# Ten places for gathered expert rows in all four tiles, with the stick-breaking core's buffers laid into the choice's buffers

## The chip, the cores and the metric

The kernel runs on one core of one Trainium2 chip. The metric is the device time of one execution in microseconds (us); smaller is better. The core has TensorE (PE), VectorE (DVE), ScalarE (ACT), GpSimd (POOL) and SyncE (SP), which run their own instruction streams and meet through semaphores, and 16 DMA engines that all queues share.

## The reference, cut to what matters

Two transformer blocks stand one behind the other, on one sequence of 256 tokens with 1024 features. The first (band attention, a short convolution, a gated feed-forward part, two layers) isn't touched. The second has two layers as well: an mLSTM mixer in layer 0, stick-breaking attention in layer 1, and behind each mixer a layer of retrieved experts:

```python
def peer_ffn(h, w_q, sub_keys, peer_u, peer_v):      # for each block of 128 tokens
    q = einsum('td,de->te', xb, w_q)                 # 8 heads x 2 halves x 128
    s = einsum('thpk,pnk->thpn', q, sub_keys)        # scores of 2 x 128 keys
    s_top, i_top = top_k(s, 16)
    cand = s_top[0][:, None] + s_top[1][None, :]     # 16 x 16 candidates
    g_top, pos = top_k(cand, 16); expert = cand_idx[pos]
    u, vv = peer_u[expert], peer_v[expert]           # 16384 experts, 1024 floats each
    act = gelu(einsum('thkd,td->thk', u, xb))
    return einsum('thk,thkd->td', softmax(g_top) * act, vv)
```

So each token takes 8 x 16 = 128 experts in each of the two layers. The stick-breaking mixer computes, for 16 heads, z = q k, log(1 - sigmoid(z)) summed over the later keys, and a = exp(log sigmoid(z) + that sum), which weighs v.

## The kernel before

**Tiles and rows.** There are two blocks of 128 tokens and two layers, so four tiles: tile 0 and 1 are layer 0, tile 2 and 3 are layer 1. A tile has 128 picks (`PICKS`). Pick q of the whole program (0 to 511) means: GpSimd gathers for each of 128 tokens one row of 2048 floats (u and v of one expert side by side, 8 KB) by an indirect DMA (L1718); VectorE multiplies the u half with the token's row and sums it (`dot`, L2457); ScalarE makes the gelu, multiplies it with the softmax weight and writes a diagonal matrix (L1530, L1533, L1539), two picks at a time; TensorE multiplies the diagonal with the v half and adds it up in PSUM (`weighted`, L1124).

**Places.** A gathered row lies in a place until TensorE has used it. `ROW[q]` says which one. Places 0 to 3 are `ring_b`, 4 to 7 are `ring_a`, the upper half of the weight ring `wring`. In tile 0 there are two more, 8 and 9: `spare`, and the first half of `qp0`, a buffer of queries that is free by then. They exist in tile 0 only: `spare` and `qp0` are allocated in an early stack that is closed and overlaid by the buffers of the second layer's mixer, among them `az`, `sp_`, `ls` and `ex` of 4 KB a partition each. So tile 0 has ten places and tiles 1 to 3 have eight. `EARLIER[q]` is the pick that had the place before; GpSimd waits for `rows_free` to reach it (L1715), then issues. GpSimd does nothing else at this time.

**What runs beside the rows.** The rows of tile 0 run beside the end of layer 0 and the choice of tile 1's experts. The second layer comes in two passes (`second_layer(t)`, in the text first and second pass), one for each block of tokens. The first pass runs beside the rows of tile 1 and ends with the choice for tile 2; the second runs beside the rows of tile 2 and ends with the choice for tile 3. Tile 3's rows run alone. A pass is: a norm; six slabs of weights for k, v and q (`tile_rows`, L1144); the norm of the heads; the core, in which groups of heads go through scores (TensorE), logarithms (ScalarE) and sums (VectorE and TensorE); two slabs of w_out, one right behind the other; a norm; four slabs of w_q (L1238); the scores of the keys (L998, copied to `sc` at L1677); and the choice (`choose`: the maxima L2362, indices L2367, and so on), all on VectorE. The 16 heads go through the core in 4 groups in the first pass and in 8 in the second.

**The order of the work** is written by hand. `PLAN` gives for each step of a pass the number of picks by which dots (VectorE, `picks`), gelus (ScalarE, `gelus`) and products (TensorE, `weighted`) must have come before the engine goes on with the next step. An engine thus waits for a row when the plan's count asks for one that hasn't landed. The plan of tile 1: 2 picks before the norm, 3 at each of the six slabs, 24 in the core, 3 + 3 around w_out, 2 before the next norm, 3 at each slab of w_q, 5 before the choice and 41 inside it; the plan of tile 2 has 40 in the core, 2 instead of 3 at w_out and w_q, and 31 in the choice. The indices of the next tile's first 64 picks are ready halfway through the choice, those of the other 64 at its end; GpSimd waits for them (`chosen`) before pick 0 and 64 of a tile.

**Weights.** The slabs of the second layer (2 MB each) go by SP's queue into the two lower places of `wring` (L541); a load is issued when the slab two before it has been used. They take the same DMA engines as the gathers.

**The buffers of the change.** `cand` (8 heads x 256 candidates, 8 KB a partition) and `sc` (16 x 128 scores, 8 KB) are used from the copy of the queries (`qpt` is a view of `cand`, L1673) to the end of the choice. `az`, `sp_`, `ls`, `ex` are used from the pass's first norm (`hkT` is a view of `ex`) to the end of the core; `krow` and `qrow` are views of `sp_` and `ls`. ScalarE writes eight diagonals in turn (`DIAGS`).

Of the kernel before, what the change touches and what calls it, by code (L numbers as in the profile page):

```python
# [8 lines left out]
F32 = mybir.dt.float32  # L9
# [8 lines left out]
P = 128  # L18
D = 1024
SEQ = 256  # L20
NT = SEQ // P
KC = D // P
DEPTH = 2
# [55 lines left out]
PICKS = PEER_HEADS * TOPK  # L79
RING = 8  # L80
HALF_RING = RING // 2


TEN, EIGHT = (0, 1, 2, 3, 8, 9, 4, 5, 6, 7), (6, 7, 0, 1, 2, 3, 4, 5)
ROW = [TEN[q % 10] if q < PICKS else EIGHT[q % RING] for q in range(DEPTH * NT * PICKS)]
EARLIER = [[p for p in range(max(0, q - 10), q) if ROW[p] == ROW[q]][-1:] for q in range(len(ROW))]
TURN = [ROW[:q + 1].count(ROW[q]) for q in range(len(ROW))]
PART = 2
LAST = DEPTH * NT * PICKS - 1
# [72 lines left out]
def build(nc, ins, out):  # L162
    ctx = ExitStack()
    with ctx:
# [6 lines left out]
        def sb(name, shape, dt=F32, stack=ctx):  # L171
            return stack.enter_context(nc.sbuf_tensor(name, shape, dt))
# [121 lines left out]
        def se(name, shape, dt=F32):  # L294
            return sb(name, shape, dt)
# [3 lines left out]
        cand = se("cand", [P, PEER_HEADS, TOPK * TOPK])  # L299
        sc = se("sc", [P, 2 * PEER_HEADS, NKEYS])  # L300
# [19 lines left out]
        def row(q):  # L320

            r = ROW[q]
            if r == RING:
                return spare[:, :]
            if r > RING:
                return qp0[:, 0].rearrange("p h n -> p (h n)")
            return (ring_b, ring_a)[r // HALF_RING][:, r % HALF_RING, :]

        early = ExitStack()
        sc1 = sb("sc1", [P, 2 * PEER_HEADS, NKEYS], F32, early)  # L330
        qp0 = sb("qp0", [P, NT, 2 * PEER_HEADS, P], F32, early)
        spare = sb("spare", [P, 2 * D], F32, early)
        early.close()

        qpt = cand[:, :, :].rearrange("p h (a n) -> p (h a) n", a=2)
# [2 lines left out]
        def sk(name, shape, dt=F32):  # L338
            return sb(name, shape, dt)
# [4 lines left out]
        vrow = sk("vrow", [P, NT, D])  # L344
        skT = sk("skT", [P, KC, SEQ])
        srs, sss = sk("srs", [P, SB_HEADS]), sk("sss", [P, SB_HEADS])
        az, sp_, ls, ex = [sk(n, [P, 2, 512]) for n in ("az", "sp_", "ls", "ex")]


        hkT = ex[:, :, :].rearrange("p a n -> p (a n)").rearrange("p (k n) -> p k n", n=P)  # L350
# [214 lines left out]
        def _(pe):  # L565
# [549 lines left out]
            def weighted(tt, k, late=True):  # L1115

                while multiplied_rows[0] < tt * PICKS + (multiplied(k) if late else k):
                    q = multiplied_rows[0]
                    multiplied_rows[0] += 1
                    if q % PICKS == 0 and tt:  # L1120
                        pe.wait_ge(sums_read, tt)
                    pe.wait_ge(diag_ready, q + 1)
                    for half in range(2):
                        m = nc.tensor.matmul(pr[half][:, :], diag[:, q % DIAGS, :], row(q)[:, D + half * 512:D + (half + 1) * 512],  # L1124
                                             start=(q % PICKS == 0), stop=(q % PICKS == PICKS - 1))
                        if q == LAST and half == 0:
                            m.then_inc(sums_full, 1)
                    m.then_inc(rows_free, 1)
                if k == PICKS:
                    pe.drain().then_inc(sums_full, 1)  # L1130
# [559 lines left out]
        @block.gpsimd  # L1690
        def _(pool):
            pool.wait_ge(w_in_slot[0], 16)
            pool.dma_start(mask8[:, :, :], ins["c_mask8"]).then_inc(const_in, 16)
            pool.dma_start(cs[:, :, :, :], ins["c_cs"]).then_inc(const_in, 16)
            pool.dma_start(adab[:, :], ins["ada_bias"]).then_inc(adab_in, 16)
            pool.wait_ge(c_ready, 1)

            with pool.Fori(0, ADA_CHUNKS // 2) as i:
                for a in range(2):
                    pool.wait_ge(ada_free, 2 * i + a + 1)  # L1700
                    pool.sem_inc(wait_seen, 1)
                    pool.dma_start(aring[:, a, :], ins["ada_rows"][bass.ds(2 * i + a, 1)].rearrange("a p n -> p (a n)")).then_inc(ada_in[a], 16)  # L1702

            for tt in range(DEPTH * NT):
                for p in range(PICKS):
                    q = tt * PICKS + p
                    if q == TEN.index(9):
                        pool.wait_ge(sc_ready, 4)
                    for r in range(2):
                        if q == TEN.index(HALF_RING + 2 * r):  # L1710
                            pool.wait_ge(w_free, S2 + SLOTS_B - 3 + r + R)
                    for i, (_, h0, _) in enumerate(CHOICES[tt]):
                        if p == h0 * TOPK:
                            pool.wait_ge(chosen, CHOICES_BEFORE[tt] + i + 1)
                    for p0 in EARLIER[q]:  # L1715
                        pool.wait_ge(rows_free, p0 + 1)
                    pool.sem_inc(wait_seen, 1)
                    pool.indirect_dma_start(out=row(q), out_offset=None, in_=ins["peer_uv"],  # L1718
                                            in_offset=bass.IndirectOffsetOnAxis(ap=eidx[:, tt % NT, p:p + 1], axis=0)).then_inc(row_in[ROW[q]], 16)


        @block.vector
        def _(dve):
# [730 lines left out]
            def dot(q):  # L2454

                dve.wait_ge(row_in[ROW[q]], 16 * TURN[q])
                m = nc.vector.tensor_tensor_reduce(out=row(q)[:, 0:D], in0=row(q)[:, 0:D], in1=hrow[:, q // PICKS % NT, :], scale=1.0,  # L2457
                                                   scalar=0.0, op0=ALU.mult, op1=ALU.add, accum_out=dots[:, q % PICKS:q % PICKS + 1])
                if q % PART == PART - 1 or q >= PAIRED:
                    m.then_inc(dots_ready, 1)  # L2460
# [208 lines left out]
```

## Time and profile before

| what | value |
|---|---|
| runs of the kernel before | 2644.65 us median of 3 (2629.52 to 2653.48) |
| profiled execution | span 2638.4 us from first to last instruction, 6.25 us under that median; no separate time of it is given |
| TensorE, VectorE, ScalarE, GpSimd busy | 88%, 66%, 37%, 26% of the span |
| gathers (software queue) | 90000 packets, 595.97 MB |
| HBM read | 824.95 MB, 313 GB/s over the span |
| tile 0's rows | from about 1155 us |
| first pass, second pass, tile 3 alone | 1511 to 1908, 1908 to 2320, 2320 to 2630 us |

The profile is of one execution; all times in rows are us from its start. PE is TensorE's matmuls, PEld its weight loads. In a row of the timeline the bracket holds how long the engine was idle before the instruction and what ended the idle time. The chain of waits is followed back from the last instruction, at each step to what released it or to the instruction before it on its engine. The granted clock of TensorE was 0.983 of full speed over the span.

### The profile page before, as it was taken

The numbers are of one execution on the slowest core, as the hardware profiler recorded it, in microseconds if no ns is written. First come the engines' busy times: TensorE is split into PE (matmuls) and PEld (weight loads), VectorE is DVE, ScalarE is ACT, GpSimd is POOL, SyncE is SP. The second block draws the span as 40 slices with busy tenths as digits, with TensorE's granted clock in tenths as the row PEclk, the third lists the DMA queues.
The fourth block names the chain that finished last, engine by engine and source line by source line (L and its number), as shares of the span: only waits on it lengthen the run. The fifth ranks groups of instructions, "written<-read, shape, count | busy, mean of one in ns | idle before, by whom it ended". The sixth has DMA issues, their size and how long they took to land.

```text
span 2638.4 us, 33375 instructions
## 1 busy us (share of the span) xinstructions
PE 2328.1 (88%) x11926; PEld 1622.5 (61%) x11926; DVE 1728.6 (66%) x3439; ACT 972.9 (37%) x2088; POOL 682.4 (26%) x631
## 2 busy tenths in 40 slices
PE   8999999999999999898877799987798999777777
PEld 7999999899999979785322244463343446232222
DVE  5687677768677767666975555547954654954444
ACT  4444433453443345322322224413324732322222
POOL 0000001000000100023545433324423333455543
PEclk9999999999999999999999999999999999899999
DMA  7545477664547754169999999999999998999998
GB/s 298 199 160 196 163 277 282 249 246 155 193 148 279 284 196 160 68 236 382 403 419 422 421 411 391 401 390 407 413 401 373 395 395 325 383 412 421 422 421 354
DMA packets 110513, 828.14 MB, mean 314 GB/s; under 512 B 14384, under 2 KB 15296, under 8 KB 30992
## 3 DMA queue, kind: packets, MB, share of 16 engines
q0 software_dynamic: 90000, 595.97, 56.1%
q1 hardware_dynamic: 20352, 230.08, 23.2%
q8 instruction: 94, 1.54, 0.2%
q14 instruction: 67, 0.55, 0.1%
HBM read 824.95 MB, written 1.05 MB: 313 GB/s over the span
## 4 chain that ended last, share of the span: by engine, by line
PE 54%; DMA 18%; DVE 14%; ACT 5%; issue 4%; POOL 1%; DVEq 1%; ACTq 1%; PEldq 0%; SPq 0%; PEld 0%; POOLq 0%
PE pd L573 16%; PE pr L1124 12%; PE pa L573 11%; DMA ring_b<-in_peer_uv,eidx 9%; DMA wring<-in_peer_uv,eidx 6%; PE pr L573 6%; PE pa L1144 3%; DVE ring_b L2457 3%; PE pa L1238 2%; DVE wring L2457 2%; DVE wring_r L1774 1%; PE pd L1144 1%; DMA wring<-in_w_mix 1%; ACT junk L1539 1%; DMA aring<-in_ada_rows 1%
## 5 line engine op out<-in xcount | busy, mean ns | idle before, releaser
L1124 PE MATMUL pr<-ring_b,junk 128*128 128x512 f32 x976 | 464.2, 622 | 112.2 <-ACT junk L1539 111.6
L1124 PE MATMUL pr<-wring,junk 128*128 128x512 f32 x968 | 451.4, 611 | 105.2 <-ACT junk L1539 99.8
L1718 POOL DMA_INDIRECT ring_b<-in_peer_uv,eidx x244 | 294.4, 1207 | 597.1 <-PE pr L1124 348.3
L2457 DVE CUSTOM_DVE_ANT_0 wring<-wring,hrow 128x1024 f32<-128x1024 f32 x242 | 293.7, 1223 | 218.9 <-DMA wring<-in_peer_uv,eidx 210.9
L2457 DVE CUSTOM_DVE_ANT_0 ring_b<-ring_b,hrow 128x1024 f32<-128x1024 f32 x244 | 295.8, 1224 | 201.6 <-DMA ring_b<-in_peer_uv,eidx 195.3
L1124 PEld LDWEIGHTS pr<-ring_b,junk 128*128 128x128 f32 x976 | 184.3, 197 | 373.9 <-issue 197.2
L1124 PEld LDWEIGHTS pr<-wring,junk 128*128 128x128 f32 x968 | 178.3, 192 | 360.8 <-issue 188.1
L1718 POOL DMA_INDIRECT wring<-in_peer_uv,eidx x242 | 291.8, 1206 | 417.3 <-PE pr L1124 359.1
L1530 ACT ACTIVATE gel<-dots 128x2 f32<-128x2 f32 x255 | 51.6, 203 | 657.2 <-DVE dots L2457 655.4
L1702 POOL DMA_DIRECT2D aring<-in_ada_rows x112 | 60.2, 538 | 871.1 <-DVE adal L1867 870.9
L573 PE MATMUL pd<-hhi,wring_r 128*128 128x256 f32 x1024 | 222.1, 281 | 0.0
L1774 DVE TENSOR_TENSOR wring_r<-wring,wtop 128x2048 fp32r<-128x2048 f32 (+1 forms) x78 | 176.4, 2263 | 58.0 <-ACT wtop L1268 55.4
L1774 DVE TENSOR_TENSOR wring_r<-wring,wring_r 128x2048 fp32r<-128x2048 f32 (+1 forms) x77 | 173.8, 2262 | 36.0 <-ACT wring_r L1268 33.3
L1539 ACT ACTIVATE junk<-ident,gel 128x128 f32<-128x128 f32 x510 | 176.8, 394 | 18.4 <-issue 1.0
L1268 ACT CAST wring_r<-wring 128x2048 fp32r<-128x2048 f32 x80 | 149.3, 1883 | 71.0 <-DMA wring<-in_w_mix 28.7
L1268 ACT CAST wtop<-wring 128x2048 fp32r<-128x2048 f32 x80 | 148.9, 1881 | 67.1 <-DMA wring<-in_w_back 25.4
L573 PEld LDWEIGHTS pd<-hhi,wring_r 128*128 128x128 f32 x1024 | 170.7, 189 | 0.0
L573 PE MATMUL pa<-flo_b,wring_r 128*128 128x256 f32 x768 | 166.9, 284 | 0.0
L1867 DVE CUSTOM_DVE_ANT_0 aring<-aring,crow 128x1024 f32<-128x1024 f32 x112 | 136.5, 1219 | 12.3 <-DMA aring<-in_ada_rows 12.0
L573 PEld LDWEIGHTS pa<-flo_b,wring_r 128*128 128x128 f32 x768 | 128.7, 190 | 4.0 <-issue 4.0
L1533 ACT ACTIVATE gel<-gel,wexp 128x1 f32<-128x1 f32 x510 | 122.7, 287 | 18.7 <-issue 1.4
L573 PE MATMUL pd<-hhi,wtop 128*128 128x256 f32 x384 | 108.6, 283 | 2.9 <-DVE hlo_r L1817 2.9
(393 smaller groups left out, 4358.7 us busy)
## 6 DMA issues: line engine op xcount, KB each, us to landing
wring<-in_w_mix SPq DMA_DIRECT2D x38, 2048.0 KB, 8.7
aring<-in_ada_rows POOLq DMA_DIRECT2D x112, 512.0 KB, 5.3
wring<-in_w_stick SPq DMA_DIRECT2D x24, 2048.0 KB, 9.4
wring<-in_w_ffn SPq DMA_DIRECT2D x22, 2048.0 KB, 8.7
wring<-in_w_lstm SPq DMA_DIRECT2D x12, 2048.0 KB, 8.3
wring<-in_w_back SPq DMA_DIRECT2D x8, 2048.0 KB, 8.5
wring<-in_w_back SPq DMA_DIRECT2D x4, 1536.0 KB, 6.8
ring_b<-in_peer_uv,eidx POOLq DMA_INDIRECT x244
```

The lines of the kernel that those rows point to most:

```text
L573: m = nc.tensor.matmul(out_, lhsT, rhs, start=start, stop=stop)
L1124: m = nc.tensor.matmul(pr[half][:, :], diag[:, q % DIAGS, :], row(q)[:, D + half * 512:D + (half + 1) * 512], start=(q % PICKS == 0), stop ...
L1144: i = nc.tensor.matmul(b[:, :], src(k), wring[:, m % R2, k, :], start=(k == 0), stop=(k == KC - 1))
L1238: i = nc.tensor.matmul(b[:, c * P:(c + 1) * P], wring[:, m % R2, k, c * P:(c + 1) * P], hT[:, k, cut], start=(k == 0), stop=(k == KC - 1))
L1268: nc.scalar.copy(hi, raw).then_inc(whi_ready, 1)
L1533: nc.scalar.activation(gel[:, i:i + 1], gel[:, i:i + 1], ACT.Copy, scale=wexp[:, g * PART // PICKS % NT, i // TOPK, i % TOPK:i % TOPK + 1])
L1539: nc.scalar.activation(diag[:, q % DIAGS, :], ident[:, :], ACT.Copy, scale=gel[:, q % PICKS:q % PICKS + 1]).then_inc(diag_ready, 1)
L1702: pool.dma_start(aring[:, a, :], ins["ada_rows"][bass.ds(2 * i + a, 1)].rearrange("a p n -> p (a n)")).then_inc(ada_in[a], 16)
L1718: pool.indirect_dma_start(out=row(q), out_offset=None, in_=ins["peer_uv"], in_offset=bass.IndirectOffsetOnAxis(ap=eidx[:, tt % NT, p:p + 1 ...
L1774: nc.vector.tensor_tensor(lo, raw, hi, ALU.subtract).then_inc(wlo_ready, 1)
L1867: nc.vector.tensor_tensor_reduce(out=aring[:, j % 2, :], in0=aring[:, j % 2, :], in1=crow[:, :], scale=1.0, scalar=0.0, op0=ALU.mult, op1= ...
L2457: m = nc.vector.tensor_tensor_reduce(out=row(q)[:, 0:D], in0=row(q)[:, 0:D], in1=hrow[:, q // PICKS % NT, :], scale=1.0, scalar=0.0, op0=A ...
```

## The change

All tiles use ten places. Place 8 is the second half of a new buffer `ring_c` and place 9 its first half, except in tile 0, where place 9 stays in `qp0`. `ring_c` takes the 16 KB a partition where the four core buffers lay; these become views of `cand` (`az`, `sp_`) and `sc` (`ls`, `ex`), each with the shape it had. `spare` goes. `ROW` now turns through the ten places over all 512 picks, and each pick's predecessor is the one ten before; nothing else is changed, no wait and no plan count.

```diff
@@ -81,9 +81,10 @@
-TEN, EIGHT = (0, 1, 2, 3, 8, 9, 4, 5, 6, 7), (6, 7, 0, 1, 2, 3, 4, 5)
-ROW = [TEN[q % 10] if q < PICKS else EIGHT[q % RING] for q in range(DEPTH * NT * PICKS)]
-EARLIER = [[p for p in range(max(0, q - 10), q) if ROW[p] == ROW[q]][-1:] for q in range(len(ROW))]
+TEN = (0, 1, 2, 3, 8, 9, 4, 5, 6, 7)
+PLACES = len(TEN)
+ROW = [TEN[q % PLACES] for q in range(DEPTH * NT * PICKS)]
+EARLIER = [[q - PLACES] if q >= PLACES else [] for q in range(len(ROW))]
 TURN = [ROW[:q + 1].count(ROW[q]) for q in range(len(ROW))]
@@ -321,15 +322,14 @@
             r = ROW[q]
             if r == RING:
-                return spare[:, :]
+                return ring_c[:, 1]
             if r > RING:
-                return qp0[:, 0].rearrange("p h n -> p (h n)")
+                return qp0[:, 0].rearrange("p h n -> p (h n)") if q < PICKS else ring_c[:, 0]
             return (ring_b, ring_a)[r // HALF_RING][:, r % HALF_RING, :]
 
         early = ExitStack()
         sc1 = sb("sc1", [P, 2 * PEER_HEADS, NKEYS], F32, early)
         qp0 = sb("qp0", [P, NT, 2 * PEER_HEADS, P], F32, early)
-        spare = sb("spare", [P, 2 * D], F32, early)
         early.close()
@@ -344,7 +344,15 @@
         srs, sss = sk("srs", [P, SB_HEADS]), sk("sss", [P, SB_HEADS])
-        az, sp_, ls, ex = [sk(n, [P, 2, 512]) for n in ("az", "sp_", "ls", "ex")]
+        ring_c = sk("ring_c", [P, 2, 2 * D])
+
+        def pair_in(v, i):
+
+            h = v[:, i * v.shape[1] // 2:(i + 1) * v.shape[1] // 2, :]
+            return h.rearrange("p (a h) n -> p a (h n)", a=2)
+
+        az, sp_ = pair_in(cand, 0), pair_in(cand, 1)
+        ls, ex = pair_in(sc, 0), pair_in(sc, 1)
```

## Rows read from the trace of the kernel before

**Rows 1.** Page, part 2: GB/s moved in each of 40 slices of 66 us.
```profile
GB/s 298 199 160 196 163 277 282 249 246 155 193 148 279 284 196 160 68 236 382 403 419 422 421 411 391 401 390 407 413 401 373 395 395 325 383 412 421 422 421 354
```

**Rows 2.** Windows: stretch; PE, PEld, DVE, ACT, POOL busy us; PEclk, DMA share, GB/s.
```profile
1375.00:1500.00 125.00, 92.51 (x200) 35.93 (x200) 61.66 (x100) 34.10 (x125) 62.68 (x50) 1.00 1.01 421
1500.00:2325.00 825.00, 719.54 (x2208) 356.25 (x2208) 516.51 (x1252) 290.46 (x804) 301.57 (x260) 0.97 0.97 391
2325.00:2600.00 275.00, 207.57 (x447) 81.29 (x448) 136.21 (x223) 76.31 (x277) 141.45 (x112) 0.99 1.01 421
```

**Rows 3.** Windows, same columns: two stretches in which fewer bytes come.
```profile
2195.00:2225.00 30.00, 29.79 (x178) 22.24 (x178) 9.74 (x27) 8.71 (x26) 6.47 (x7) 1.00 0.70 249
2275.00:2300.00 25.00, 20.80 (x40) 8.11 (x38) 23.90 (x101) 8.33 (x23) 12.03 (x10) 0.86 0.87 319
```

**Rows 4.** Chain of waits, 1500 to 2325: start us, us, what; all transfers.
```profile
1485.20 17.53 DMA wring<-in_peer_uv,eidx
...
1616.92 8.38 DMA ring_b<-in_peer_uv,eidx
...
1706.08 9.99 DMA wring<-in_peer_uv,eidx
...
1797.81 9.24 DMA ring_b<-in_peer_uv,eidx
...
1817.74 11.68 DMA ring_b<-in_peer_uv,eidx
...
1870.87 9.08 DMA wring<-in_peer_uv,eidx
...
2154.43 9.26 DMA ring_b<-in_peer_uv,eidx
...
2233.59 12.25 DMA wring<-in_peer_uv,eidx
```

**Rows 5.** Timeline, first pass, after w_out: DVE waits, then PE waits.
```profile
1713.64 1.23 DVE L2457 CUSTOM_DVE_ANT_0 wring<-wring,hrow 128x1024 f32<-128x1024 f32 x1 [6.68 <-DMA wring<-in_peer_uv,eidx]
...
1720.86 1.54 PE L903 MATMUL pd<-ident,xn 128*128 128x128 f32 x6 [5.28 <-DVE xn L2166]
```

**Rows 6.** Timeline at the start of the choice: first pass, then second.
```profile
1789.75 0.58 ACT L1677 COPY sc<-pa 128x512 f32<-128x512 f32 x1 [0.31 <-PE pa L998]
...
1792.78 1.23 DVE L2457 CUSTOM_DVE_ANT_0 wring<-wring,hrow 128x1024 f32<-128x1024 f32 x1 [7.06 <-DMA wring<-in_peer_uv,eidx]
...
1793.93 1.25 DVE L2362 MAX8 top<-sc 128x8 f32<-128x128 f32 x6
...
2219.08 0.58 ACT L1677 COPY sc<-pa 128x512 f32<-128x512 f32 x1 [0.31 <-PE pa L998]
...
2221.26 1.64 DVE L2362 MAX8 top<-sc 128x8 f32<-128x128 f32 x8
```

**Rows 7.** Waits of DVE, 1793 to 1910, then 2221 to 2325: us, times, longest.
```profile
DVE wring L2457 <- DMA wring<-in_peer_uv,eidx: 9.2, 5, 7.1
...
DVE ring_b L2457 <- DMA ring_b<-in_peer_uv,eidx: 1.7, 4, 0.8
...
DVE wring L2457 <- DMA wring<-in_peer_uv,eidx: 6.4, 2, 6.1
...
DVE ring_b L2457 <- DMA ring_b<-in_peer_uv,eidx: 1.1, 2, 0.7
```

**Rows 8.** Timeline of DVE at the start of the first core.
```profile
1625.33 1.23 DVE L2457 CUSTOM_DVE_ANT_0 ring_b<-ring_b,hrow 128x1024 f32<-128x1024 f32 x1 [1.22 <-DMA ring_b<-in_peer_uv,eidx]
```

**Rows 9.** Chain of waits in the last tile's rows: one transfer.
```profile
2391.62 12.56 DMA ring_b<-in_peer_uv,eidx
```

**Rows 10.** Weight loads (L541): landing times; then PE around the second pass's w_q.
```profile
DMA to landing us min/median/max: 7.9/9.4/12.8
...
2178.89 3.70 PE L1124 MATMUL pr<-ring_b,junk 128*128 128x512 f32 x8
...
2193.36 7.31 PE L1238 MATMUL pa<-hT,wring 128*128 128x128 f32 x64
```

## The prediction, as it went on record before the changed kernel ran

> **What bounds the kernel now.** The page comes first. Its bytes per slice [rows 1] show where the change acts: from the 19th slice on, when experts' rows are gathered, the core moves 325 to 422 GB/s, and no slice passes 422. I read this as a ceiling of the transfers with dips under it. The windows say how deep the dips are [rows 2]. In the first of its three stretches (tile 0, ten places) and in the third (the last tile alone, eight places) the rate is 421 GB/s. Between them, in the 825 us in which the two passes of the second layer run beside tiles 1 and 2, it is 391. A row gather moves 128 rows of 2048 floats, 1.049 MB, so one takes 2.49 us at 421 GB/s. If the middle stretch ran at 421, it would be (421 - 391) / 421 x 825 = 58.8 us shorter. That is the ceiling of anything that only keeps the transfers busier.
>
> The ceiling is not what more places bring. The chain of waits says which wait ended last [rows 4]: between 1500 and 2325 us it holds eight transfers, and all the rest is TensorE, VectorE and ScalarE. The first one belongs to tile 0. From 1880 to 2154 us none is on the chain at all: there the rows lie ready before they are used. So the middle stretch is mostly bound by the engines, whose work is interleaved with the rows by the plan's counts, and the missing 30 GB/s are mostly the transfers waiting for a free place. In the last tile it is the other way: all of its rows come at 2.49 us each, and the end is set by when the last gather lands.
>
> **What a place is worth.** A place is busy from the issue of its gather until TensorE has multiplied its row. Under the ceiling eight places make a turn of 8 x 2.49 = 19.9 us, of which 12.56 are the transfer [rows 9]; ten make 24.9 us, of which 17.53 are the transfer (the first row of [rows 4]). The rest, some 7.3 us, is the same. So in a stretch that the transfers bound, ten places give a longer queue and no more rows per second: that is what rows 2 show side by side. Two more places help only around a stretch in which TensorE or VectorE is late: the transfers can then run two rows further ahead, which is worth at most 2 x 2.49 = 5.0 us each time the work turns from engine-bound to transfer-bound.
>
> **The change part by part.**
>
> Tile 0 keeps its ten places and its order; only one address moves. 0 us. Rows 128 to 133 have rows ten earlier as their predecessors before and after, so the turn to tile 1 gains nothing.
>
> The shared buffers: no instruction, wait or DMA is added or taken away, and the four core buffers keep their shapes. The choice of the next experts and the core of the same pass are ordered by engine queues already. Cost 0; nothing queues behind anything new. Had a hidden order been broken, waits would be needed that the diff doesn't have.
>
> (a) After w_out in the first pass. Two slabs run on TensorE back to back with no rows between, all eight places fill, and VectorE then needs the ninth and tenth row for its plan: it sits 6.68 us for the first of them, and TensorE 5.28 us for the norm behind them [rows 5]. Both rows would be in the two added places. VectorE's wait goes; TensorE, which multiplies older rows until then, is next to be late, so the gain is its 5.28: **5.3 us**. Bounds: 0 if TensorE takes longer over the rows it now has in hand, 6.7 if it too starts earlier.
>
> (b) Before the choice in the first pass VectorE waits 7.06 us for a row and starts the maxima at 1793.93, while the scores were there at 1789.75 + 0.58 = 1790.33 [rows 6]. With the row issued two places sooner the scores are next: **3.5 us** (0 to 3.6).
>
> (c) The same place in the second pass: 2221.26 - (2219.08 + 0.58) = **1.6 us** (0 to 1.6) [rows 6].
>
> (d) Inside the two choices, where VectorE is the busy engine, it still waits for rows: 9.2 - 7.1 + 1.7 = 3.8 us and 6.4 - 6.1 + 1.1 = 1.4 us [rows 7], the longest one being that of (b) and (c). VectorE is close to being the bound, and part of what it gains is waited for later. I take half of 5.2: **2.6 us** (0 to 5.2).
>
> (e) The cores. The one transfer on the chain there ends in a wait of 1.22 us [rows 4, 8]. **1.2 us** (0 to 5.0, two rows).
>
> (f) The turn into the last tile. From 2275 to 2300 us the transfers move 319 GB/s, so they idle (421 - 319) / 421 x 25 = 6.1 us [rows 3] because all places are taken. With two more they fetch two rows in that time, and since nothing but transfers bounds what follows, the end comes 2 x 2.49 = **5.0 us** earlier (0 to 5.0). This is the surest term.
>
> Elsewhere the dips are engine-bound on both sides; the deepest, 2195 to 2225 us at 249 GB/s with TensorE busy 29.79 of 30 us [rows 3], can't get shorter.
>
> Sum: 5.3 + 3.5 + 1.6 + 2.6 + 1.2 + 5.0 = 19.2 us. The profiled execution has a span of 2638.4 us; the median of the three runs shown is 2644.65, 6.25 us above. 2638.4 - 19.2 = 2619.2 for a span, and 2644.65 - 19.2 = **2625.5 us** for the time (0.7% less). About 1% is what a measurement of this kernel can tell from no change, so this would be hard to see.
>
> **The rivals.**
>
> 1. *Hidden anyway* (0.25). The engines' chain has other waits of nearly the same length beside each row wait, so (a) to (e) vanish and at most (f) stays: a gain of 0 to 5, time 2640 to 2645. For it: TensorE is busy 720 of the 825 us [rows 2]. Against: at (a) and (b) both the waiting and the next-late engine are visible. The same result follows if the transfers themselves can't do more in the middle stretch than they do: then the time is 2645. Against it: 421 GB/s held for 125 and for 275 us [rows 2].
> The Trainium skill ("SBUF — State Buffer", section "A bandwidth-pool intuition that's wrong") puts the HBM side at about 358 GB/s per core. By that rule 391 would be past the limit already, and no extra place could bring anything; the trace disagrees, with 421 GB/s on this one core.
>
> 2. *Every dip shrinks* (0.17). If the engines' stages are themselves held up by rows throughout, each dip loses up to two rows. From 58.8 take what two rows can't cover: the stretch 2195 to 2225 idles 30 x (421 - 249) / 421 = 12.3 us, so 7.3 remain, and 1.1 of the 6.1 us at 2275. Gain 50, time about 2594. Against: only seven transfers of this stretch are on the chain.
>
> 3. *Slower: the weights come late* (0.05). Each 2 MB slab shares the transfers with the rows in flight, and more rows would be ahead of it. Room is least around w_q in the second pass: a slab is freed at 2178.89 and its successor needed at 2193.36, 14.5 us, and the longest landing of any slab is 12.8 us [rows 10]. If slabs waited behind all rows in flight, ten would make 24.9 + 5.0 = 29.9 us, 15.4 too late for two slabs: +31 us, 2676. It decides from a landing of 14.5 us on. Against: by the same reckoning eight places would give 24.9 us now, and the longest is 12.8.
> The Trainium skill ("DMA: Bandwidth & Descriptors", section "Queues, rings and completion order") says that each DMA engine takes turns between its queues, a packet at a time. By that rule a deeper gather queue doesn't push the slabs back, the price is 0 and the time stays at the sum; the landings of 7.9 to 12.8 us agree.
>
> 4. *It doesn't do what it says* (0.03): the rows come in the old rhythm because something else (the index choice for the next tile, the eight diagonals) holds the gathers; time 2645.
>
> **How the numbers follow.** The forecast, a gain of 12 to 28 us, gets 0.50; the rivals 0.25, 0.17, 0.05 and 0.03. The 1% bound lies at 26.4 us: faster by more is rival 2 and the upper edge of the forecast, 0.22. Slower by over 1% is rival 3 and a little for what I can't see, 0.05. The rest, 0.73, is within 1%. The range 2600 to 2648 takes in the forecast (2617 to 2633), rival 1, and the nearer part of rival 2.
>
> **What would show it.** Right: the middle stretch runs at 396 to 402 GB/s, with the last tile still at 421; the transfer in a saturated turn takes about 17.5 us in all tiles; TensorE's 5.28 us wait for the norm is gone and the maxima start within 0.5 us of the last score copy; the window of 25 us before the last tile moves over 400 GB/s; slab landings stay under 14 us. Wrong: the 6.68 and 7.06 us waits are still there (rival 4) or gone without the stage getting shorter (rival 1), TensorE waits for slabs (rival 3), or the middle stretch is over 30 us shorter (rival 2).

## The result, and the profile after

| | before | after |
|---|---|---|
| runs | 2639.44 us median of 20 (2629.52 to 2657.13) | 2617.75 us median of 20 (2609.43 to 2635.95) |
| ratio after / before | | 0.9923, 95% interval 0.9907 to 0.9939 |
| profiled execution, span | 2638.4 us | 2611.3 us |

The change gains 0.77%, 20.3 us of 2639.4 by the ratio, between 16 and 25 us by its interval. The forecast was a gain of 19.2 us. The two profiled executions differ by 27.1 us in span. That is more than the runs say. Executions of one kernel differ with the granted clock (of the 20 of after, the fastest took 2609.43 us at 0.989 and the slowest 2635.95 at 0.976; one of e_plan10, below, with 3883.59 us at 0.553, is left out of its ratio). So the stages below are used for where the time went, and the ratio for how much.

The page after, part 2, GB/s in each of 40 slices, now 65 us long:

```profile
GB/s 298 204 159 201 162 282 282 241 237 160 191 165 271 271 237 162 33 224 369 401 418 422 421 422 410 417 409 414 421 424 390 395 392 347 418 398 421 422 422 353
```

Against [rows 1] the ceiling is the same, 424 at most, and the slices from the 24th to the 30th have filled up: 390 to 413 before, 409 to 424 now. The deep dip near the end (325 before) is still there (347). The three stretches of [rows 2], after; the columns are the same:

```profile
1375.00:1500.00 125.00, 92.19 (x200) 35.74 (x199) 61.65 (x100) 34.44 (x125) 63.57 (x50) 1.00 1.01 421
1500.00:2300.00 800.00, 705.82 (x2202) 350.60 (x2201) 511.23 (x1246) 288.69 (x798) 304.98 (x260) 0.98 0.98 404
2300.00:2575.00 275.00, 207.71 (x453) 81.47 (x452) 139.58 (x229) 78.44 (x285) 147.56 (x114) 1.00 1.01 421
```

The outer stretches stay at 421 GB/s. The middle one moves the same bytes (391 x 825 and 404 x 800 agree within 0.2%) in 25 us less, with nearly the same number of instructions (2202 products for 2208). Its busy TensorE time falls by 13.7 us, more than six products of less than half a us each explain, and its granted clock is 0.98 instead of 0.97. That last pair is not in the forecast, and comes back below.

The chain of waits after, 1500 to 2330 us, all of its transfers (start us, us):

```profile
1800.85 14.63 DMA wring<-in_peer_uv,eidx
...
1851.45 14.67 DMA wring<-in_peer_uv,eidx
...
2311.69 11.15 DMA wring<-in_peer_uv,eidx
```

Seven transfers of [rows 4] after tile 0's have become three, two in the first choice and one at the turn into the last tile. The one that is gone from the second pass, issued at 2154.43 in [rows 4], comes back below too. In the last tile a transfer takes 17.5 us where it took 12.56 [rows 9], as in tile 0 before: one row of the same view, 2340 to 2500 us.

```profile
2355.02 17.52 DMA wring<-in_peer_uv,eidx
```

**Where the time went.** I cut each profiled execution at the starts of named instructions and took the differences, in us. A stage in which nothing changed still comes out 1.7 or 3.4 us apart now and then: from the first to the last of the six slabs of the second pass it is 67.5 or 70.9 us, with one value in between, in an order that has nothing to do with the places (eight places have 70.9, but also 67.5). The rows show what the steps are. The same rows' products, behind the same wait of 2.01 us for a diagonal, in before and then in after:

```profile
1954.89 5.40 PE L1124 MATMUL pr<-wring,junk 128*128 128x512 f32 x8 [2.01 <-ACT junk L1539]
```

```profile
1941.41 3.70 PE L1132 MATMUL pr<-ring_b,junk 128*128 128x512 f32 x8 [2.01 <-ACT junk L1547]
```

Before has 5.40 us twice in these slabs, at a granted clock of 0.89 over 1945 to 1960 us and 0.88 over 1974 to 1988; after has 3.70 both times, at 1.00. From 1500 us on each of the two traces has six such waits of 2.01 us; a slow stretch follows three of them in before and one in after. So about 1.7 us behind such a wait are there in one execution and not in another, and a single difference of that size needs a row behind it.

In the table "nine", "twelve late" and "six" are e_nine, e_twelve and e_six of the experiments.

| stage | eight (before) | eight (e_layout) | nine | ten (after) | twelve late | six |
|---|---|---|---|---|---|---|
| pass 1: last w_out slab to first w_q slab | 37.2 | 38.1 | 33.3 | 30.3 | 30.2 | 40.7 |
| pass 1: first core scores to the next slab | 64.9 | 64.9 | 64.9 | 64.9 | 64.9 | 73.4 |
| pass 1: last w_q slab to first maxima | 20.9 | 21.6 | 19.1 | 17.4 | 17.4 | 26.0 |
| first choice, to tile 1's last sum | 114.5 | 117.2 | 116.6 | 113.1 | 113.5 | 132.0 |
| pass 2: core | 110.0 | 110.0 | 110.0 | 110.0 | 110.0 | 119.4 |
| pass 2: last w_out slab to first w_q slab | 29.3 | 29.2 | 27.3 | 27.3 | 27.2 | 35.9 |
| pass 2: first to last w_q slab | 34.5 | 34.5 | 32.9 | 32.9 | 32.9 | 32.9 |
| pass 2: key scores to first maxima | 6.0 | 5.9 | 4.5 | 4.5 | 4.5 | 13.4 |
| second choice, to tile 2's last sum | 99.0 | 99.4 | 98.2 | 97.3 | 98.9 | 100.3 |
| last tile, to its last sums | 312.9 | 313.0 | 310.5 | 308.0 | 303.0 | 351.7 |

Before against after: 6.9, 0, 3.5, 1.4, 0, 2.0, 1.6, 1.5, 1.7 and 4.9 us. That is 23.5 of the 27.1, and 3.2 more than the ratio gives; 3.4 are the scatter of the second pass's six slabs, 2.0 lie ahead of tile 0's end, where nothing differs, and the rest, of either sign, is spread over the other stages.

Three places, seen in rows. TensorE after w_out in the first pass, of after (start us, us):

```profile
1709.88 3.60 PE L1132 MATMUL pr<-ring_b,junk 128*128 128x512 f32 x8
1713.32 1.04 PE L911 MATMUL pd<-ident,xn 128*128 128x128 f32 x8
1714.19 3.60 PE L1132 MATMUL pr<-ring_b,junk 128*128 128x512 f32 x8
```

and of before, at the same place, with the row of the products that follow:

```profile
1720.86 1.97 PE L903 MATMUL pd<-ident,xn 128*128 128x128 f32 x8 [5.28 <-DVE xn L2166]
1722.61 4.28 PE L1124 MATMUL pr<-wring,junk 128*128 128x512 f32 x8
```

(L1132 is L1124 of before, L911 is L903.) The wait of 5.28 us is gone. But so are 0.9 us of the norm's products and 0.7 of the rows' (1.97 to 1.04, 4.28 to 3.60). The window 1720 to 1723 us of before shows the granted clock at 0.59:

```profile
1720.00:1723.00 3.00, 2.15 (x9) 2.10 (x10) 2.96 (x4) 0.00 (x0) 0.00 (x0) 0.59 0.99 412
```

After 5.28 us of idleness the engine goes on for part of these 3 us at the lower of its two levels (1.2 instead of 2.4 GHz, half speed). The gap costs 5.28 + 1.6 = 6.9 us.

ScalarE's last score copy and VectorE's first maxima in the first pass, of after:

```profile
1780.75 0.58 ACT L1685 COPY sc<-pa 128x512 f32<-128x512 f32 x1 [0.31 <-PE pa L1006]
1781.41 1.65 DVE L2370 MAX8 top<-sc 128x8 f32<-128x128 f32 x8 [3.88 <-ACTq L1686]
```

The maxima start 0.08 us after the copy's end, where they started 3.6 later [rows 6]. VectorE still idles 3.88 us, but now for the scores and no longer for a row.

The second pass, where I had named no gain: TensorE from the rows' products to the first w_q slab, of before, then the slab of after.

```profile
2163.22 3.70 PE L1124 MATMUL pr<-wring,junk 128*128 128x512 f32 x8 [0.64 <-ACT junk L1539]
2166.76 1.04 PE L991 MATMUL pa<-ident,hT 128*128 128x128 f32 x8
2169.77 9.01 PE L1238 MATMUL pa<-hT,wring 128*128 128x128 f32 x64 [1.97 <-ACT hrow L1499]
```

```profile
2152.32 7.38 PE L1246 MATMUL pa<-hT,wring 128*128 128x128 f32 x64 [0.89 <-ACT hrow L1507]
```

VectorE in the second pass of before, between its norm and the modulated rows that the slab needs (its waits for rows there):

```profile
2158.20 1.23 DVE L2457 CUSTOM_DVE_ANT_0 wring<-wring,hrow 128x1024 f32<-128x1024 f32 x1 [0.27 <-DMA wring<-in_peer_uv,eidx]
2160.68 1.23 DVE L2457 CUSTOM_DVE_ANT_0 wring<-wring,hrow 128x1024 f32<-128x1024 f32 x1 [1.25 <-DMA wring<-in_peer_uv,eidx]
2163.71 1.23 DVE L2457 CUSTOM_DVE_ANT_0 ring_b<-ring_b,hrow 128x1024 f32<-128x1024 f32 x1 [0.51 <-DMA ring_b<-in_peer_uv,eidx]
```

These are 2.0 us, and in after VectorE does the same steps, from 2142.38 to 2148.77 us, without a wait for a row.

### The profile page after: what moved, and what is told of

Read it like the earlier page. It is cut to its first block, busy times and chain, and to the rows that moved or that the text cites. A ratio compares the mean times of both kernels' runs of the same rounds, so it can differ in the third digit from the quotient of the medians.

```text
span 2611.3 us, 33375 instructions
## 1 busy us (share of the span) xinstructions
PE 2312.3 (89%) x11926; PEld 1614.5 (62%) x11926; DVE 1727.1 (66%) x3439; ACT 972.3 (37%) x2088; POOL 689.0 (26%) x631
## 3 DMA queue, kind: packets, MB, share of 16 engines
q8 instruction: 94, 1.54, 0.2%
## 4 chain that ended last, share of the span: by engine, by line
PE 56%; DMA 16%; DVE 15%; ACT 5%; issue 4%; DVEq 1%; POOL 1%; ACTq 1%; PEldq 0%; SPq 0%; PEld 0%; POOLq 0%
PE pd L581 16%; DMA wring<-in_peer_uv,eidx 14%; PE pr L1132 12%; PE pa L581 11%; PE pr L581 8%; PE pa L1152 3%; DVE wring L2465 3%; PE pa L1246 2%; DVE ring_b L2465 1%; DVE wring_r L1782 1%; DMA wring<-in_w_mix 1%; PE pd L1152 1%; POOL wring L1726 1%; ACT junk L1547 1%; DVE ring_c L2465 1%
## 5 line engine op out<-in xcount | busy, mean ns | idle before, releaser
L1132 PE MATMUL pr<-wring,junk 128*128 128x512 f32 x816 | 381.6, 613 | 93.7 <-ACT junk L1547 90.0
L1132 PE MATMUL pr<-ring_b,junk 128*128 128x512 f32 x824 | 383.0, 610 | 89.8 <-ACT junk L1547 88.3
L1726 POOL DMA_INDIRECT ring_b<-in_peer_uv,eidx x206 | 245.6, 1192 | 517.9 <-PE pr L1132 272.6
L2465 DVE CUSTOM_DVE_ANT_0 ring_b<-ring_b,hrow 128x1024 f32<-128x1024 f32 x206 | 249.6, 1224 | 154.4 <-DMA ring_b<-in_peer_uv,eidx 149.6
L1132 PEld LDWEIGHTS pr<-wring,junk 128*128 128x128 f32 x816 | 150.9, 193 | 309.1 <-issue 159.8
L1726 POOL DMA_INDIRECT wring<-in_peer_uv,eidx x204 | 254.5, 1247 | 331.6 <-PE pr L1132 285.5
L1132 PEld LDWEIGHTS pr<-ring_b,junk 128*128 128x128 f32 x824 | 152.4, 193 | 304.4 <-issue 162.1
L2465 DVE CUSTOM_DVE_ANT_0 wring<-wring,hrow 128x1024 f32<-128x1024 f32 x204 | 246.6, 1223 | 132.5 <-DMA wring<-in_peer_uv,eidx 126.8
L1132 PE MATMUL pr<-ring_c,junk 128*128 128x512 f32 x356 | 170.6, 620 | 43.1 <-ACT junk L1547 41.0
L1276 ACT CAST wring_r<-wring 128x2048 fp32r<-128x2048 f32 x80 | 149.3, 1883 | 70.5 <-DMA wring<-in_w_mix 27.3
L2465 DVE CUSTOM_DVE_ANT_0 ring_c<-ring_c,hrow 128x1024 f32<-128x1024 f32 x89 | 108.2, 1224 | 86.0 <-DMA ring_c<-in_peer_uv,eidx 83.2
L1726 POOL DMA_INDIRECT ring_c<-in_peer_uv,eidx x89 | 112.0, 1259 | 157.4 <-PE pr L1132 142.2
L1132 PEld LDWEIGHTS pr<-ring_c,junk 128*128 128x128 f32 x356 | 66.2, 195 | 138.3 <-issue 70.9
## 6 DMA issues: line engine op xcount, KB each, us to landing
wring<-in_w_stick SPq DMA_DIRECT2D x24, 2048.0 KB, 11.6
```

What stands on the lines that cost most here:

```text
L1276: nc.scalar.copy(hi, raw).then_inc(whi_ready, 1)
```

## The experiments

Every kernel was timed against the kernel before on the same chip; "gain" is 2639 us times (1 - ratio). e_warm20 was run once, e_six, e_nine and e_sixteen four times each.

**Buffers alone.** The buffers of after, eight places from tile 1 on:

```diff
-ROW = [TEN[q % PLACES] for q in range(DEPTH * NT * PICKS)]
+EIGHT = (6, 7, 0, 1, 2, 3, 4, 5)
+ROW = [TEN[q % 10] if q < PICKS else EIGHT[q % 8] for q in range(DEPTH * NT * PICKS)]
... (EARLIER: the last pick with the same place)
```

> The buffers of the changed kernel, but eight places from tile 1 on, as before. My theory (all of the gain comes from the two places): the time of the kernel before, ratio 0.998 to 1.002; TensorE's wait of 5.3 us for the norm after w_out and VectorE's 7 us wait before the first choice are back. Rival (where the core's buffers lie matters): 0.7% faster, as the changed kernel, or part of it, with shorter core stages.

Measured: 2638.31 us, ratio 1.000 (0.9983 to 1.0018), and the wait is back, in the timeline of TensorE of this kernel:

```profile
1720.18 1.97 PE L911 MATMUL pd<-ident,xn 128*128 128x128 f32 x8 [4.99 <-DVE xn L2174]
```

VectorE waits 8.24 us before the first choice. So the shared buffers cost and gain nothing that an interval of 5 us either way or the stages show, and the gain belongs to the places.

**One half each.** e_first has ten places in tiles 0 and 1 and eight from pick 256 on; e_second has eight in tile 1 and ten from pick 256 on. In both, `EARLIER` is the last pick with the same place.

```diff
+# e_first: EIGHT = (4, 5, 6, 7, 0, 1, 2, 3)
+ROW = [TEN[q % 10] if q < 2 * PICKS else EIGHT[q % 8] for q in range(DEPTH * NT * PICKS)]
+# e_second
+LATE = (8, 9, 6, 7, 0, 1, 2, 3, 4, 5)
+ROW = [TEN[q % 10] if q < PICKS else EIGHT[q % 8] if q < 2 * PICKS
+       else LATE[(q - 2 * PICKS) % 10] for q in range(DEPTH * NT * PICKS)]
```

> Ten places in tiles 0 and 1, eight from tile 2 on. My theory: the terms of the first pass alone: from the second slab of w_out to the first of w_q 30.3 us instead of 37.2, from the key scores to the maxima 4.5 instead of 8.0, the first choice some 1.4 shorter; second pass, its choice and the last tile as before (6.0 us to the maxima, about 312.9 us from the end of tile 2 to the last sums). Sum about -12 us, ratio 0.9955. Rival (the gain is the queue's depth at the turn into the last tile): -5 us or less is missing here, everything in the second half.

> Eight places in tile 1, ten from tile 2 on. My theory: -1.5 us before the second choice, -1.7 in it, -4.9 in the last tile (308.0 us instead of 312.9), and up to 2 after w_out of the second pass: -8 to -10 us, ratio 0.9965; the first pass as before (37.2 and 8.0 us). Rival (each dip shrinks by two rows): more than -15 us here, since the deepest dips lie in the second pass.

Measured: e_first 0.9952 (0.9933 to 0.9972), a gain of 12.6 us; e_second 0.9958 (0.9943 to 0.9973), 11.1 us. Together 23.7, which the interval of the whole change (16 to 25) holds: the halves add up. The stages agree but for one: e_first has 30.3 and 17.4 us in the first pass and the values of eight places behind it (29.2, 34.5, 6.0, 312.8), e_second the reverse (37.4 and 21.0; then 27.3, 32.9, 4.5, 308.4). The exception is the first choice, which was to be 1.4 us shorter in e_first and takes the 114.5 us of before. The second choice does follow the places (97.3 us in e_second, about 99 in e_first).

**How many places.** Nine places and six places in tiles 1 to 3, the buffers of after:

```diff
+NINE = (6, 7, 0, 1, 2, 3, 8, 4, 5)      # e_nine; e_six: SIX = (6, 7, 0, 1, 2, 3)
+ROW = [TEN[q % 10] if q < PICKS else NINE[(q - PICKS) % 9] for q in range(DEPTH * NT * PICKS)]
... (EARLIER as above)
```

> Nine places from tile 1 on. New theory: the last tile takes 310.4 us, half way between 312.9 and 308.0; after w_out in the first pass VectorE still waits for one row of the two, which lands 2.5 us sooner: 34 to 35 us instead of 37.2; before the first choice the row wanted is released by the same pair of products as with eight, so nothing is gained (21 us from key scores' start of the slab to the maxima, not 17.4). Ratio 0.996 to 0.998. Rival (only a pair of places counts, since picks go in twos): as with eight places.

Measured: 2623.73 us, 0.9932 (0.9914 to 0.995). The last tile takes 310.5 us and the stage after w_out 33.3: about halfway. Before the choices one more place was already enough (4.5 us from key scores to maxima in both passes); a gain there was not expected. In the first pass it doesn't last: with the first choice added, nine places take 19.1 + 116.6 = 135.7 us, as eight do (135.4), and ten take 130.5. The ratio gives e_nine 17.9 us (13 to 23), more than was expected (5 to 11) and more than its stages add up to; with four executions it can't be told apart from the 20.3 of ten places.

> Six places from tile 1 on, buffers as in the changed kernel. My theory: the last tile stays near the ceiling (a turn of 6 x 2.49 = 14.9 us just holds a transfer of 7.6 and the 7.3 us from landing to release), at 405 to 421 GB/s; the waits for rows before the norm and before the choices grow by about one turn of two rows each, and rows of 3 per slab now run short at the slabs too: 25 to 50 us slower than before. Rival (the engines bound the passes, places hardly matter): less than 15 us slower.

Measured: 2752.64 us, 1.0428 (1.0395 to 1.0461), 113 us slower. Missed by far. The chain of waits in its last tile (start us, us) shows one turn of a place:

```profile
2472.28 9.29 DMA ring_b<-in_peer_uv,eidx
2481.59 1.23 DVE ring_b L2465
2484.14 2.00 PE pr L1132 x4
2486.93 0.94 POOL ring_b L1726
2488.65 9.10 DMA ring_b<-in_peer_uv,eidx
```

A turn is 16.4 us, 9.3 of them the transfer; I had let the transfer fall to 7.6, and in this turn it doesn't. That is no shortest time of a single gather. The view of all 512 gathers of e_six has:

```profile
DMA to landing us min/median/max: 5.3/9.0/19.7
```

Places come free two at a time, when TensorE has used a pair of rows, and in this tile the first gather of a pair takes about 8.5 us and the second 9.3. Why they take that long with, on average, only some three in flight (6 x 8.9 / 16.4), no run takes apart. Six rows per 16.4 us are 2.73 us a row, and the window of this stretch shows it:

```profile
2400.00:2700.00 300.00, 217.03 (x438) 84.67 (x437) 134.48 (x218) 75.74 (x275) 129.99 (x110) 0.94 0.97 384
```

384 GB/s instead of 421. The last tile alone is 38.8 us longer than with eight places; the other 74 are spread, also over stages that two places more than eight do not shorten (both cores +8.5 and +9.4 us; the first choice has +17.5). So eight places reach the ceiling when nothing disturbs, and six no longer do; seven were not run.

**The gap or the rows?** If the 6.9 us after w_out are all TensorE's idleness, keeping its clock up brings back only a part. Products whose result nobody reads are put into the gap of the kernel before, 30 calls in e_warm and 20 in e_warm20:

```diff
                 weighted(tt, at["fnorm"])
+                if t == 0:
+                    idle_products(30)
                 pe.wait_ge(txn_ready, NT + 2 * t + 2)
```

> The kernel before, with 30 products of the identity (about 0.13 us each, 3.9 us) ahead of TensorE's wait for the norm after w_out in the first pass. Theory (an idle gap of TensorE costs its own length and then a stretch at the lower of its two clock levels): the wait that is left is 1.3 us or less, the transposes behind it take 1.04 us instead of 1.97 and the eight products after them 3.60 instead of 4.28; from the second slab of w_out to the first of w_q 35.6 us instead of 37.2. Rival (the 1.6 us came from the rows or from other causes): 37.2 stays. The time changes by 0.1% at most either way.

> The kernel before with 20 idle products ahead of TensorE's wait for the norm after w_out in the first pass; with 30 they took 6.86 us and ran over the wait by 1.6 us. 20 take 4.6 us and end before the norm is there. Theory (the lower clock level comes after the idle gap): transposes 1.04 us, first eight products 3.60 us, and 35.6 us from the second slab to the first of w_q. Rival: 37.2 us.

Measured: e_warm 0.9991 (0.9969 to 1.0013); its 30 calls stand in the trace as 60 products (x60), took 6.86 us instead of the expected 3.9 and overran the gap, so that what the clock gave back was lost to them (36.9 us for the stage). e_warm20, one execution, span 2636.3 us, TensorE's timeline:

```profile
1712.62 4.63 PE L666 MATMUL pa<-ident 128*128 128x128 f32 x40
1717.61 1.09 PE L903 MATMUL pd<-ident,xn 128*128 128x128 f32 x8 [0.37 <-DVE xn L2168]
1718.54 3.60 PE L1124 MATMUL pr<-wring,junk 128*128 128x512 f32 x8
```

The norm and the rows' products run at full speed (1.09 and 3.60 us; 1.04 and 3.60 in e_warm), and the stage takes 35.8 instead of 37.2: 1.4 us are the clock's, the rest of the 6.9 is the wait itself. The window of this kernel over the same instructions has the clock at 1.00:

```profile
1717.00:1720.00 3.00, 2.63 (x15) 1.72 (x14) 3.00 (x6) 0.12 (x1) 0.00 (x0) 1.00 1.02 426
```

**The plan instead of the places.** If the row comes too late after w_out only because the plan wants it there, the plan could want it earlier: four rows more before w_out in the first pass and two in the second, one row instead of three (in the second pass two) at each of its slabs, in the kernel before (e_plan8) and after (e_plan10).

```diff
-    out, q, step = ((3, 3, 41), (2, 2, 31))[t]
+    o, out, q, step = ((6, 1, 3, 41), (4, 1, 2, 31))[t]
...
-    ... + [("o", 2), ("out0", out), ("out1", out), ...
+    ... + [("o", o), ("out0", out), ("out1", out), ...
```

> The kernel before with eight places and the same moved counts. Theory: four rows are used and their places filled again ahead of the two slabs, so the ninth and tenth row are there in time: TensorE's 5.3 us wait and the slow stretch behind it go without any added place, 5 to 7 us faster than before in the first pass (37.2 to about 30.5), 1 to 3 in the second; nothing else changes, ratio 0.996 to 0.998. Rival (only more places help): no change, 37.2 us.

> The changed kernel, with the plan's counts around w_out moved: 6 picks ahead of its slabs and 1 + 1 behind them in the first pass (2 and 3 + 3 in the changed kernel), 4 and 1 + 1 in the second (2 and 2 + 2). Theory: with ten places no wait for rows is left there, TensorE has the same work in another order: within 2 us of the changed kernel. Rival (the 17.3 us in which GpSimd issues nothing cost something even with ten places): 3 us or more faster.

Measured: e_plan8 1.0004 (0.998 to 1.0029), e_plan10 0.9927 (0.9898 to 0.9957). e_plan8 was expected 5 to 7 us faster in the first pass, and isn't. Its stage after w_out falls from 37.2 to 26.4 us, but the core ahead of it grows from 64.9 to 74.1 and the slab between from 7.4 to 9.1: 109.5 before, 109.6 now. The wait has only moved. With ten places the plan of before is not worse either: after has 64.9 + 30.3, e_plan10 70.8 + 27.5 = 98.3, three us more. Both stages together get shorter only with more places.

**More than ten.** Two more places from pick 342 on (two buffers that are free by then), and in e_sixteen four more from pick 356 on, in the lower half of the weight ring:

```diff
+FROM = 342
+LATE = (10, 11) + tuple(TEN[(FROM + i) % 10] for i in range(10))
+ROW = [TEN[q % 10] if q < FROM else LATE[(q - FROM) % 12] for q in range(DEPTH * NT * PICKS)]
+EARLIER = [([p for p in range(max(0, q - 12), q) if ROW[p] == ROW[q]][-1:] or [q - 12]) if q >= 10 else [] for q in range(len(ROW))]
...
+            if r == 10:
+                return vrow[:, :, :].rearrange("p t d -> p (t d)")
+            if r == 11:
+                return skT[:, :, :].rearrange("p k s -> p (k s)")
+# e_sixteen: r > 11 -> wring[:, 0:R2], one row in each quarter
```

> The changed kernel, with two more places (the values' and the keys' buffers of the core, free by then) from pick 86 of tile 2 on, that is after w_out of the second pass: twelve in w_q, the second choice and the last tile. My theory (the turn into the last tile has at most 1.1 us of idle transfers left, the stages before it are the engines'): 0 to 2 us faster than the changed kernel, ratio to the kernel before 0.990 to 0.993, last tile 306.5 to 308.0 us. Rival (each turn gives another two rows): 5 us faster, last tile 303.

> As the version with twelve places from pick 86 of tile 2 on, with four more from pick 100 on, in the two slab buffers that w_q's last slabs have left: sixteen in most of the second choice and in the last tile. New theory (each place that is filled while the engines are behind stays a row ahead until the last tile, which the transfers bound, so it is worth 2.49 us at the end, as 312.9, 308.0 and 303.0 us with eight, ten and twelve show): last tile 293 us, 10 us less than with twelve, ratio to the kernel before 0.985 to 0.988; where the transfers find no more idle time in the choice (twelve left some 5 us of it), the gain stops at about 5: 298 us. Rival (the second gain of 5 us with twelve was an accident of phase): last tile 303 or 308 us.

Measured: e_twelve 2612.03 us, 0.990 (0.987 to 0.993); e_sixteen 2612.7 us, 0.9902 (0.9886 to 0.9919). Both ratios are below that of the change (0.9923), but the intervals touch its interval, so that is not settled by the runs; their profiled spans are 2609.8 and 2605.4 against 2611.3 us. The last tile is clear: 308.0 with ten, 303.0 with twelve, 299.6 with sixteen, where I had expected 306.5 to 308.0 and then 293 or, with no idleness left, 298. Part of it is given back ahead of it: the second choice takes 98.9 us with twelve or sixteen and 97.3 with ten, for a reason that no run shows. I had held that little idleness of the transfers was left at the turn. The windows in the second choice say otherwise. After:

```profile
2270.00:2280.00 10.00, 6.21 (x14) 2.20 (x12) 9.17 (x33) 4.50 (x10) 5.70 (x5) 1.00 0.99 397
2280.00:2290.00 10.00, 8.23 (x15) 3.43 (x16) 9.43 (x13) 2.45 (x9) 2.44 (x3) 0.83 0.84 337
2290.00:2300.00 10.00, 6.63 (x16) 2.53 (x15) 7.39 (x14) 2.75 (x10) 3.70 (x4) 1.00 0.97 373
```

With sixteen:

```profile
2270.00:2280.00 10.00, 7.11 (x16) 2.58 (x14) 9.17 (x36) 4.20 (x8) 6.59 (x5) 1.00 1.01 421
2280.00:2290.00 10.00, 8.21 (x13) 3.36 (x14) 9.59 (x13) 2.76 (x10) 2.29 (x2) 0.66 1.01 421
2290.00:2300.00 10.00, 7.16 (x13) 2.49 (x11) 5.82 (x14) 2.75 (x10) 3.00 (x5) 0.83 1.02 424
```

Ten places leave (421 - 369) / 421 x 30 = 3.7 us of idleness here, and (421 - 264) / 421 x 30 = 11.2 us in the dip at w_q before it. This is the dip, 2180 to 2210 us, in after and then with twelve:

```profile
2180.00:2210.00 30.00, 29.79 (x151) 19.96 (x150) 13.28 (x54) 10.09 (x31) 9.97 (x9) 1.00 0.70 264
```

```profile
2180.00:2210.00 30.00, 29.79 (x164) 21.04 (x164) 12.25 (x46) 10.09 (x31) 8.31 (x8) 1.00 0.87 338
```

Twelve places move 338 GB/s there, (338 - 264) x 30 = 2.2 MB more, two rows. TensorE is just as busy and its work takes no less time, and the last tile is two rows' time shorter. That the lead of these very rows is carried through the choice to the end is the reading that fits, not a thing that a row shows. At sixteen the transfers hardly idle from 2220 us on (419 GB/s or more in each 10 us), and the next two pairs of places bring 3.4 us together and no longer 5 each.

## Why the prediction was right or wrong

**The whole.** 2625.5 us was forecast and 2617.75 measured, a gain of 19.2 us against 20.3 by the ratio. The forecast stood on the median of the three runs first shown, 2644.65; the 20 runs have 2639.44, and 5.2 of the 7.8 us between forecast and result are that base. 404 GB/s in the middle is a little above the 396 to 402 that were named, and belongs to a profiled execution that gained 27 us, not 20.

That the sum came out so near is in part luck. By stages (a) had 1.6 us too little, 3.6 us in the second pass had no term, (e) had 1.2 too much, and the stages add up to 23.5 us where the ratio has 20.3. "Hard to see", with 1% as what a measurement can tell, was too pessimistic: 20 executions of each kernel give an interval of 0.9907 to 0.9939, clear of no change.

**(a) After w_out: 5.3 forecast, 6.9 measured.** The mechanism held: VectorE's wait went, and TensorE's 5.28 with it. Too small was the price of the gap. The prediction counted only the idle time, and not that the engine works at its lower level behind it; 1.54 for 6 of the norm's products stood in [rows 5] and should have been compared with the 1.04 for 8 of them elsewhere. e_warm20 shows that part alone, 1.4 us.

**(b), (c) Before the choices: 3.5 and 1.6 forecast, 3.5 and 1.5 measured.** Bounding the gain by what is late next (the last score copy) came out, since that copy ends the wait now. (c) repeats itself (5.8 to 6.0 us in all executions profiled with eight places, 4.5 with ten). The figure of (b) depends on the pair of executions: against e_layout the stage gains 4.2 us.

**(d) Inside the choices: 2.6 forecast, 1.4 + 1.7 = 3.1 measured.** Near, but the 1.4 of the first choice is not above the scatter of one execution (e_layout, with eight places, has 117.2 us where before has 114.5, and e_first, with ten, has 114.5 as well). The 1.7 of the second returns in e_second (97.3 us). The half was a choice between 0 and 5.2, and the runs neither confirm nor refute it for the first choice. Firmer is (b) with the first choice added: 135.4, 138.8 and 136.2 us with eight places (before, e_layout, e_second), 130.5, 130.9 and 131.9 with ten (after, e_twelve, e_first).

**(e) The cores: 1.2 forecast, 0 measured.** The first core takes 64.9 us with eight, nine, ten and twelve places (tiles 0 and 1 of e_twelve have ten). The wait of 1.22 us on the chain [rows 8] had others beside it. Over the first core VectorE's waits for rows fall from 7.6 to 1.3 us, its waits for TensorE's sums grow from 9.3 to 11.6, and TensorE waits 5.6 us for diagonals both times. So an earlier row only made VectorE wait elsewhere, and here rival 1 was right. With six places the core does lengthen, so rows matter there, but the reserve of eight is enough.

**(f) The turn into the last tile: 5.0 forecast, 4.9 measured**, two places at 2.49 us. e_nine (2.4) confirms the price of one. What was wrong is the remainder: rival 2 was priced as if 1.1 of 6.1 us were left, and "can't get shorter" was said of the dip at w_q. True of the engines' work in the dip, false, by e_twelve, of what the dip is worth: with two more rows fetched in it the transfer-bound tile is 5.0 us shorter. e_sixteen adds 3.4.

**What was missed.** 2.0 + 1.6 us in the second pass, from w_out to the end of the first w_q slab. "Elsewhere the dips are engine-bound on both sides" was too quick. The sum had no term for the seventh transfer of [rows 4]: issued at 2154.43, it lands at 2163.69, VectorE waits for it, and the chain goes on over the modulated rows to the first w_q slab. VectorE's three waits for rows there are the 2.0 us. TensorE then idled 1.97 us ahead of the slab, where it idles 0.89 in after, and did the slab in 9.01 instead of 7.38 us. The window of the slab in the kernel before has the clock at 0.82:

```profile
2166.00:2174.00 8.00, 6.03 (x36) 5.29 (x35) 4.26 (x8) 2.33 (x7) 1.87 (x2) 0.82 1.02 423
```

The window of after, over the same part of its slab, has it at 1.00 and more work done:

```profile
2148.60:2156.60 8.00, 7.11 (x51) 5.81 (x50) 6.16 (x11) 2.33 (x7) 3.46 (x3) 1.00 1.01 421
```

e_second, which has ten places from tile 2 on, shows the same 27.3 us, 7.38 us for the slab and no transfer on the chain there; e_first has the 29.2 of before, 9.01 us and the transfer. The 2.0 us are so shown to be the places'. The 1.6 of the clock are less certain: of five executions with eight places and the plan of before, four have the slab in 9.01 us, behind 1.97 to 2.16 us of idleness, and e_warm has it in 7.38 behind 1.65. e_plan8, with eight places, has 0.90 and 7.38. That fits a slab that depends on the idleness ahead of it, which two places shorten, and not on the number of places itself.

**The rivals.** Rival 1 (hidden anyway) holds for the cores alone. The Trainium skill's 358 GB/s per core ("SBUF — State Buffer", section "A bandwidth-pool intuition that's wrong"), by which nothing could be gained, does not hold for this one core: it moves 421 to 424 GB/s in e_sixteen, and places brought time. Rival 2 (every dip shrinks) falls: the bytes of the middle stretch take 25 us less in the profiled execution, not 50. Rival 3 falls. The weight loads, after:

```profile
DMA to landing us min/median/max: 8.4/11.6/12.8
```

The median rose by 2.2 us from [rows 10] and the longest did not move, under the 14.5 us at which it would have decided. The rule that each DMA engine takes turns between its queues (the Trainium skill, "DMA: Bandwidth & Descriptors", section "Queues, rings and completion order") fits that. A load behind all the rows in flight would have landed after some 22 us, an estimate from the 17.5 us of a gather and the 5.0 of 2 MB at 421 GB/s.

## What to carry to other kernels

One more buffer is worth up to one transfer's time each time an engine-bound phase with waits turns into a transfer-bound one, as long as the transfers idle anywhere ahead of that turn, and nothing inside a saturated phase; count the idleness over the whole stretch since the last turn, not in the last window. Price a gap of TensorE as the gap plus what runs behind it at the lower level, by comparing the next rows with the same rows elsewhere; behind a gap of 2 us that second part came in some executions and not in others. Follow every transfer on the chain of waits into a term: the one that was left out was worth 2.0 us. And cap the gain of a wait by what is late next, which came out near here twice, while counting it whole where it stood beside others failed.

## What was unexpected of the hardware

In a saturated turn a gather of 1 MB takes 17.5 us with ten places, 14.5 with nine, 12.56 with eight, always the turn less 7.3 to 7.9, but with six it takes 9.3, not 7.6, and the rate falls from 421 to 384 GB/s, though single gathers of the same kernel land in 5.3. And a short idle gap of TensorE, 5.28 us, or even 1.97 us behind another of 0.64, was followed by work at a granted clock of 0.59 or 0.82, worth 1.6 us each time, which no wait in the profile shows. Behind gaps of 2.01 us it came or didn't, 5.40 or 3.70 us for the same products, and this is part of the scatter between executions of one kernel.
